# RWKV scan stage: the forward substitution's products on 64 rows instead of 32, a changed order of the work, and eight 128-row products of constants at the head of each pair

## The reference, cut to what matters

```python
def step(s, inp):
    r_t, lw_t, k_t, v_t, a_t, b_t = inp
    sa = jnp.einsum('dbhij,dbhj->dbhi', s, a_t)
    s = s * jnp.exp(lw_t)[..., None, :] + sa[..., None] * b_t[..., None, :] + v_t[..., None] * k_t[..., None, :]
    return s, jnp.einsum('dbhij,dbhj->dbhi', s, r_t)
s_fin, y = lax.scan(step, s0, (tm(r), tm(logw), tm(k), tm(v), tm(a), tm(b)))
```

## Time and profile before

| | us |
|---|---|
| median of 3 runs | 2722.91 |
| lowest and highest run | 2720.70, 2728.16 |
| profiled execution, its own time | 2720.06 |
| its span, first to last instruction | 2718.4 |
| PE busy | 2245.3 (83%) |
| PEld (weight loads) busy | 1735.0 (64%) |
| DVE busy | 984.4 (36%) |
| ACT busy | 518.1 (19%) |

### The profile page before, as it was taken

How to read it: one execution, slowest core, us unless ns; L and a number is a source line. 1 busy time by engine, 2 the same in 40 slices (tenths; PEclk the granted TensorE clock), 3 DMA queues, 4 the chain that set the end, 5 groups by cost and what they waited for, 6 DMA issues and landing times. The chain is left out here.

```text
span 2718.4 us, 39159 instructions
## 1 busy us (share of the span) xinstructions
PE 2245.3 (83%) x16630; PEld 1735.0 (64%) x16630; DVE 984.4 (36%) x2209; ACT 518.1 (19%) x920; POOL 58.2 (2%) x85
## 2 busy tenths in 40 slices
PE   1999955798999886899859993688888889779797
PEld 0888854687888775788624442466666777536445
DVE  3224346411440372675161003544544441120253
ACT  1011022401000101100110003444444333010142
POOL 0000000000000300000000000000000000000000
PEclk9999977898999898899979995776667776689889
DMA  7465410424874321775303203111101111312100
GB/s 289 173 230 228 171 64 8 86 93 165 336 280 155 124 78 37 281 302 217 138 16 109 92 31 125 38 39 38 35 15 39 29 25 41 124 66 93 52 10 16
DMA packets 103014, 305.14 MB, mean 112 GB/s; under 512 B 71352, under 2 KB 79800, under 8 KB 85184
## 3 DMA queue, kind: packets, MB, share of 16 engines
q1 hardware_dynamic: 94384, 225.11, 24.3%
q0 software_dynamic: 8464, 77.60, 7.3%
HBM read 286.88 MB, written 15.80 MB: 111 GB/s over the span
## 5 line engine op out<-in xcount | busy, mean ns | idle before, releaser
L263 PE MATMUL bank<-h,ring 128*128 128x256 f32 x2944 | 646.7, 383 | 22.8 <-DVEq L967 15.3
L263 PEld LDWEIGHTS bank<-h,ring 128*128 128x128 f32 x2944 | 566.3, 193 | 104.0 <-DVEq L967 16.0
L263 PE MATMUL bank<-mixed,ring 128*128 128x512 f32 x384 | 165.0, 592 | 1.3 <-DVE mixed L1249 1.3
L877 PE MATMUL bank<-ffn_hidden,ring 128*128 128x256 f32 x704 | 152.4, 379 | 3.3 <-PEq L903 3.3
L877 PEld LDWEIGHTS bank<-ffn_hidden,ring 128*128 128x128 f32 x704 | 133.6, 190 | 22.2 <-issue 4.1
L263 PEld LDWEIGHTS bank<-mixed,ring 128*128 128x128 f32 x384 | 72.9, 190 | 93.5 <-issue 91.4
L156 DVE CUSTOM_DVE_ANT_0 next_w<-next_w,next_vec,par 128x1024 f32<-128x1024 f32 x96 | 120.1, 1279 | 11.4 <-DMA next_w<-in_mod_stream 11.4
L1987 DVE TENSOR_TENSOR rw_u<-bank,rw_lam 128x128 f32<-128x128 f32 x120 | 35.0, 291 | 236.1 <-PE bank L1660 233.1
L889 DVE SCALAR_TENSOR_TENSOR x<-bank,mod,x 128x256 f32<-128x256 f32 x24 | 10.0, 477 | 231.6 <-PE bank L877 231.6
L1668 PE MATMUL bank<-rw_gr,rw_u 64*64 64x32 f32 x960 | 80.3, 252 | 13.0 <-DVE rw_u L1987 12.9
L1581 PE MATMUL bank<-rw_xa,ring 64*64 64x64 f32 x1024 | 30.5, 305 | 72.2 <-DVE rw_xa L1920 72.2
(11 more groups left out here) (387 smaller groups left out, 3415.1 us busy)
## 6 DMA issues: line engine op xcount, KB each, us to landing
ring<-in_stream SPq DMA_DIRECT2D x89, 2048.0 KB, 8.0
next_w<-in_mod_stream POOLq DMA_DIRECT2D x24, 2048.0 KB, 9.9
ctx<-in_mod_rest POOLq DMA_DIRECT2D x16, 1024.0 KB, 7.3
rwkv_projections<-proj_out POOLq DMA_DIRECT2D x8, 1024.0 KB, 6.7
y<-bias_table SPq DMA_DIRECT2D x48, 128.0 KB, 4.9
rw_rkv<-rwkv_projections SPq DMA_DIRECT2D x8, 768.0 KB, 4.2
rw_at<-rw_at_kept SPq DMA_DIRECT2D x16, 256.0 KB, 3.9
rwkv_o<-rwkv_projections POOLq DMA_DIRECT2D x1, 2048.0 KB, 16.0
```

What stands on the lines that cost most here:

```text
L263: mm = pe.matmul(out, ring_tile(k, n, kt, i * P), rhs[kt], start=start and kt == kts[0], stop=stop and kt == kts[-1])
L877: mm = pe.matmul(k.psum[grp * 4 + i][:, 0:T], ring_tile(k, n, kt, i * P), rhs[part * KT + kt], start=(part == 0 and kt == 0), stop=(part = ...
```

## The change

The solving products take 64 rows. A new tile `LM` for each direction holds the inverse on the partitions `brows(h)` and zeros (set once) on `krows(h)`. The load from DRAM goes into `LM` instead of `BG`, and both operands of L1618's product span `rows64(h)`. `LM` has one copy per direction, so SP waits for the products of the pair before (`pq_up`) ahead of the load. The product with the unit matrix stays on 32 rows. Room for `LM` comes from two small tiles, which now lie on constants (`tri`, `neg`).

In `steps_made` the unit products of both heads come first and then those of `rt` for both heads; their number and size stay.

The order changes by its intervals. A new item `warm` stands at the head of each step from i = -1 on: ten times eight products of 128 rows and 512 columns, of the unit matrix with constants, into the next work bank, which nobody reads.

```diff
+        order += [("warm", i, 1)] if i >= -1 else []
         order += interleave((0, 1, has(i, [("chain", i, c) for c in range(NCK + 1)])),
-                            (0, 0.7, has(i + 1, scan_solve(i + 1))),
-                            (0, 0.3, has(i + 2, scan_grams(i + 2))),
+                            (0, 0.75, has(i + 1, scan_solve(i + 1))),
+                            (0.1, 0.42, has(i + 2, scan_grams(i + 2))),
                             (0, 0.3, has(i - 1, scan_read(i - 1))),
-                            (0.3, 0.36, has(i + 2, [("bonus", i + 2, j) for j in range(2)])),
-                            (0.45, 1, has(i + 2, [("inv", i + 2, s) for s in range(1, LCH)])),
-                            (0.42, 1, has(i + 3, scan_ready(i + 3))))
+                            (0.42, 0.46, has(i + 2, [("bonus", i + 2, j) for j in range(2)])),
+                            (0.55, 1, has(i + 2, [("inv", i + 2, s) for s in range(1, LCH)])),
+                            (0.48, 0.9, has(i + 3, scan_ready(i + 3))))
...
+        LM = [sb(f"lm{d}", 8, 2, LCH) for d in range(2)]
...
+                for d in range(2):
+                    for h in range(2):
+                        nc.vector.memset(LM[d][krows(h)].rearrange("p a b t -> p (a b t)"), 0.0)
...
+                if n:
+                    sp.wait_ge(pq_up, 8 * n)
                 for d in range(2):
                     for h in range(2):
-                        sp.dma_start(BG[n % 3][d][brows(h), :, :, 96:128].rearrange("p c e t -> p (c e) t"),
+                        sp.dma_start(LM[d][brows(h)].rearrange("p c e t -> p (c e) t"),
                                      blocks(mt_dram, n, d, h)).then_inc(mt_in, 16)
...
-                        x, y = VQ[n % 2][d][brows(h), c2, e, :], KP[d][brows(h), c2, e, :]
+                        x, y = VQ[n % 2][d][rows64(h), c2, e, :], KP[d][rows64(h), c2, e, :]
...
-                        mm = pe.matmul(out[brows(h), j * P:(j + 1) * P], BG[n % 3][d][brows(h), c2, e, 96:128], both,
-                                       start=True, stop=True)
+                        mm = pe.matmul(out[brows(h), j * P:(j + 1) * P], LM[d][rows64(h), c2, e, :], both, start=True,
+                                       stop=True)
...
+                elif kind == "warm":
+                    out = take(*item)
+                    for _ in range(8):
+                        pe.matmul(out, ident, k.con[:, 0:512], start=True, stop=True)
```

More of the change, by code:

```diff
@@ L1363, in stage_rwkv_scan @@
         jobs = {"lora": [(0,), (1,)], "gram": [(0,), (1,)], "gr": [(0,), (1,)], "btok": [()],
-                "atok": [()], "akv": [()], "pq": [()],
+                "atok": [()], "akv": [()], "pq": [()], "warm": [()],
                 "kk": [()], "bonus": [()] if item[2:] == (0,) else [],
@@ L1407, in stage_rwkv_scan @@
         U, lam = sb("u", 2, 2, 64), sb("lam", 4, 2, NCK)
-        starts, gmask, sel, half2 = sb("starts", 512), sb("gmask", 64), sb("sel", 512), sb("half2", 6)
-        cen, omka, eps = sb("cen", P), sb("omka", KT), sb("eps", 1)
+        starts, gmask, sel, half2 = sb("starts", 512), const(k, "tri")[:, 0:64], sb("sel", 512), sb("half2", 6)
+        cen, omka, eps = const(k, "neg"), sb("omka", KT), sb("eps", 1)
         kst, kstT, rst, rstT = sb("kst", 8), sb("kstT", P), sb("rst", 8), sb("rstT", P)
@@ L1628, in steps_made @@
                 for h in range(2):
+                    to = [outs[h][rows64(e), 0:384].rearrange("p (c v) -> p c v", c=4) for e in range(2)]
+                    units = [ident[rows64(e), rows64(e)] for e in range(2)]
                     for e in range(2):
-                        unit = ident[rows64(e), rows64(e)]
-                        to = outs[h][rows64(e), 0:384].rearrange("p (c v) -> p c v", c=4)
+                        pe.matmul(to[e][:, :, 0:64], units[e], units[e].unsqueeze(1).to_broadcast([64, 4, 64]), start=True,
+                                  stop=False, skip_group_check=True)
+                    for e in range(2):
                         rt = RT[n % 2][d][rows64(e), 256 * half:256 * half + 256].rearrange("p (c h t) -> p c h t", h=2,
                                                                                            t=LCH)
-                        pe.matmul(to[:, :, 0:64], unit, unit.unsqueeze(1).to_broadcast([64, 4, 64]), start=True, stop=False,
+                        pe.matmul(to[e][:, :, 64:96], units[e], rt[:, :, h, :], start=False, stop=False,
                                   skip_group_check=True)
-                        pe.matmul(to[:, :, 64:96], unit, rt[:, :, h, :], start=False, stop=False, skip_group_check=True)
                 for j in range(4):
```

## The result

| | before | after |
|---|---|---|
| median, us | 2725.53 (4 runs) | 2756.67 (4 runs, 2751.59 to 2766.64) |
| profiled execution, own time and span | 2720.06, 2718.4 | 2757.0, 2755.3 |
| mean granted clock | 0.858 | 0.889 |

The recorded ratio is 1.0136, with a 95% interval of 1.0116 to 1.0157: 1.4% slower, where 2714 us was forecast. (The two medians of the table alone make 1.0114.

A forecast was written before the change was run, and what follows sets the result against it. Each pair was taken as a PE-bound head, partly at half clock, and a tail bound by DVE's inversion. Steady pairs: -4.0, 77.9 us for 81.9; whole stage: -9.1, so 2714 us; range 2700 to 2728, with rivals 2682 to 2748.

The forecast's parts named there:

- I take 7 us cold in all: Head of a steady pair: 7 us still run at half rate, work of 4 at full rate, costing +3.1 us.
- order term: Steady pair: kk 2 sums moved into the PE-bound head cost +1.1 us, `exps` between two pq items +1.0.
- Burst and boundary: Boundary of a steady pair: burst takes 8.9 us; U14 to next U0 goes from 9.1 to 12.2, +3.1.
- rival 4: DVE falls behind: the squeezed inversion costs 2 us in six pairs, giving 2726 us; chance 0.13.
- Clock at the head: Head of a steady pair: warming the 26.3 and 10.2 us cold stretches gives -15.7 us, remaining cold work +3.1.
- rival 2: The burst buys nothing: clock falls again soon after it, some 22 us cold per head, 2752 us; chance 0.24.
- rival 1: The clock stays up: both falls in the head vanish, pair 7 stays warm, 2678 to 2690, say 2684; chance 0.20.
- Solving products: The pq items: on 64 rows, unit and solving products run one after the other, 0.43 us an item, +3.4 a pair.
- Rival 3: The pq items: unit and solving products overlap still, -3.4 us in seven pairs, 2690 us; chance 0.10.
- Ends: Last pairs and read-out: pair 5 +5.2 us, pair 6 +1.1, pair 7 -3, last read-out +4.8.
- Step -1: Before the first pair: burst free behind PE's 16.7 us wait for `elements`, akv items start earlier, -3 us.
- Nothing, for want of a reason: Order of unit products, LM loads with SP's new wait, memsets and banks: claimed to change no time.

The follow-up runs named there:

- e5: Changed kernel with grams (0 to 0.3) and bonus (0.3 to 0.36) back at their old places: 2741.31 us, ratio 1.0078 to the kernel before.
- e6: Changed kernel with the kk items (`ready`) moved later, to 0.58 to 0.97 from 0.48 to 0.9: 2729.02 us, ratio 1.0050 to the kernel before.
- e13: Changed kernel with the product with the unit matrix on 64 rows as well: 2721.35 us, ratio 1.0007 to the kernel before.
- e1: Changed kernel with bursts out and the old order back, leaving solving products on 64 rows: 2716.84 us, ratio 0.9996 to the kernel before.
- e3: Changed kernel without bursts and with solving products on 32 rows, leaving the new order: 2730.24 us, ratio 1.0038 to the kernel before.
- e4: Changed kernel without the ten bursts, new order and 64-row solving products kept: 2728.93 us, ratio 1.0045 to the kernel before.
- e9: Changed kernel without bursts and with the kk items later, at 0.58 to 0.97: 2711.81 us, ratio 0.9966 to the kernel before.
- e15: Changed kernel with order, bursts and 64 rows undone, leaving tile `LM` and the gr item's order: 2727.00 us, ratio 1.0015 to the kernel before.
- e10: Changed kernel with old order and no bursts, solving and unit products both on 64 rows: 2688.50 us, ratio 0.9888 to the kernel before.
- e12: Changed kernel with the kk items later and bursts only at steps -1 to 5: 2711.40 us, ratio 0.9972 to the kernel before.
- e7: Changed kernel with no bursts at the last three heads (pairs 6 and 7, last read-out): 2744.85 us, ratio 1.0099 to the kernel before.
- e2: Changed kernel with the old order and solving products on 32 rows, leaving the ten bursts: 2741.83 us, ratio 1.0079 to the kernel before.
- e16: Changed kernel with late kk items, solving and unit products on 64 rows, bursts only up to head 5: 2687.63 us, ratio 0.9882 to the kernel before.
- e14: Changed kernel with old order and no bursts, unit products on 64 rows, solving products on 32: 2779.92 us, ratio 1.0228 to the kernel before.

## Why the prediction was wrong, point by point

Two steps failed. The clock term "I take 7 us cold in all" was mis-sized: 13.7 to 27.3 us of the heads of pairs 1 to 4 are cold. And the order term (+1.1 and +1.0) prices only what PE, ACT and DVE do; it left out SP's load of the next pair, for which PE waits 2.8 to 6.2 us a pair.

The profiled time was to be 2711.0 (2720.06 less 9.1) and is 2757.0. Of these 46.0 us, pairs 1 to 4 bring 36.5 (348.1 for 311.6), pair 0 4.9 (78.6 for 73.7), the stretch before the first U 4.7, pair 6 1.3 and the end 1.7; pair 5 and 7 came out 2.6 and 0.6 under.

- **Burst and boundary: right.** 8.5 us for 8.9; U14 to U0 11.6 for 12.2 in pair 3. DVE didn't fall behind: U12 to U14 7.7 us for 7.4, so rival 4 is out.
- **Clock at the head: wrong by the most.** "I take 7 us cold in all": it was 27.3 in pairs 3 and 4, 17.1, 17.1 and 13.7 in pairs 0 to 2 and nothing in pair 5. By the prediction's own rate, 27.3 - 7 = 20.3 us more at half rate are 20.3 x 3/7 = 8.7 us. This is rival 2, near the place that it named: the clock fell 0.7 us ahead of the akv items and stayed down through them, the chain item and the sums. It gave 2752. That this is near the measured time is in part luck: it has nothing of the load, the 64 rows did help the clock, and the run that it blamed (akv, akv, chain, sums) ends at a fall only in pair 2 (8.4 us behind U0, for 3.4 us). The trace had told of it in the earlier trace rows, where 10.20 of 10.20 busy us were cold; the working used that row against rival 1 and then spared the head all the same. What the engine did before each fall is below.
- **Order: a step left out.** The text priced what PE, ACT and DVE do in moved items and asked of SP only what the new wait does. It never asked what SP's own load of the next pair stands behind. That is 3.0 us of wait in pair 3 (0.26 before), in the text nothing; e5 and e6 put it at 16 to 23 us of the time with all that follows from it. The rows to look at were SP's timeline: load issued at 1968.00, wanted at 1973.97, and 4.5 us to land (2070.53 to 2075.07 after) leave 1.4 us of slack, against items moved by 0.1 of an 81.9 us step. Two more waits of PE are new in the head and were priced at nothing: 1.40 us for the read-out's `rw_ysb` and 1.23 us for `elements` (rows in the last section). Three old ones, 0.68, 0.84 and 0.68 us, are gone or shorter; PE's idle time from U0 to U12 of pair 3 is 6.0 us for 2.5. Whether the terms for `kk` and `exps` (+1.1 and +1.0) were right no run tells.
- **Solving products: mechanism right, price nearly so, a gain missed.** They do run one after the other: 0.54 us an item for 0.43 (1.54 less 1.00), so 4.3 a pair for 3.4. Rival 3 is out for this kernel. e13 shows what it is worth, 35 us, with what the clock does then. What the text didn't have is that 64 rows raise the clock at all ("64 rows don't lift it" was part of rival 2). The two cancel in e1.
- **Sum of pair 3.** 77.9 + 8.7 (clock) + 3.0 (load) + 0.9 (items) - 0.6 (boundary) = 89.9, and 88.6 were measured. Over pairs 1 to 4 the same terms give 24.6 + 15.7 + 3.6 - 1.2 = 42.7 us on top of the forecast, and 36.5 were measured. They account for the miss to some 6 us; as the waits just named are not in them, they are an estimate and no proof.
- **Ends: nearly right.** Pair 5 +2.6 (+5.2), pair 6 +2.4 (+1.1), pair 7 from U0 to U14 -3.6 (-3), the last read-out +6.5 (+4.8).
- **Step -1: wrong way.** The first U was to come 3 us earlier and came 1.7 later (1779.31 for 1777.59). The late load is in this step too: PE waits 7.60 us for ACT's square, for 1.30 before. With neither bursts nor the old order (e3, e4) the first U is at 1777.9. With the kk items later it is at 1774.9 with bursts (e6) and 1775.3 without (e9), but in e5, where that wait is down to 1.78 us, it is at 1780.1. No run took this stretch apart.
- **"Nothing, for want of a reason": not contradicted** for tile `LM` and the gr products (e15, within 0.4%).

By the Trainium skill ("TensorE: Matmul & The Clock Gate", Part 3) products overlap when their row groups differ, and its table of packings has products side by side in different columns too. This case's traces agree with the first for 32 and 32 rows (1.00 us) and with the second for two 64-row kinds on the same rows, whose outputs lie on different partitions (`krows(h)` and `brows(h)`) and so in different columns (e10, 1.01 us). The mix, however, has different columns as well and runs one behind the other (1.54 us); there the measurement decides, and the prediction's low end, "other columns of the array may be enough", fails for it.

What stays open: why e4 plus bursts loses 25 us when e9 plus bursts (e12) loses none. 10 of it are the last three bursts (e7). The rest goes with the wait, which is there in the one and not in the other, but no run took it apart further. Nor did any run tell what lets the clock fall, or why taller products keep it up.

## What to carry to other kernels

When items of a hand-made order move, list for every queue, SP's included, what stands behind them and by when it is wanted; a load with 1.4 us of slack doesn't survive a shift of 5. When a product is made taller, make those that ran beside it as tall: here that one line was worth 28 to 35 us; it took the whole change back to even (e13), and without the bursts and the new order it makes a kernel 1.1% faster than the one before (e10). Work added to lift the clock has to be held against what it displaces, place by place. The bursts came out even in pairs 2 to 4 of e2 and as a whole in e12 and e16; in the changed kernel they cost 25 us, 10 of them at the end.

## What the runs showed of the hardware that was not expected

- Products of 32 and of 64 rows on shared rows run one after another, whichever is the taller (1.54 us an item in e1 and e14). Two kinds with the same number of rows overlap, on disjoint rows (1.00 us before) and on shared ones (1.01 us in e10).
- A product on 64 rows, half of them meeting zeros, takes PE as long as one on 32 (0.62 and 1.06 us for the same passes in e1 and e14), and the granted clock of the same stretch was higher with it: 0.77 for 0.72, 0.89 for 0.73.
- 8.5 us of dense 128-row passes did not by themselves keep the clock up for the head behind them. In pair 3 it fell to 1.2 GHz three times before U12, and each time PE had just been idle or was so: 1.40 us until 2030.73 (fall at 2032.4), 1.23 us until 2059.53 (2059.7), 2.99 us until 2075.85 (2073.4).

```profile
2030.73 0.35 PE L1669 MATMUL bank<-rw_u,rw_gr 64*64 64x64 f32 x5 [1.40 <-DVE rw_ysb L2013]
...
2059.53 1.86 PE L1588 MATMUL bank<-rw_xa,ring 64*64 64x64 f32 x64 [1.23 <-DVE rw_xa L1933]
```

Once down it stayed so with PE busy for 13.70 of 13.70 us. Such a gap was neither enough nor needed, though. Pairs 1 and 5 have the same gap of 1.40 us behind U0 and one of 1.24 and 1.30 us near 24, and there the clock stayed up until 38.0 and 55.1 us behind U0. And in the kernel before it fell at 1998.69 with PE busy throughout, behind chain and sums items; so it did in pairs 0, 1, 3 and 4. Pair 1 of the changed kernel, then the kernel before on both sides of that fall (columns as in the earlier trace rows):

```profile
1857.90:1895.80 37.90, 33.28 (x737) 26.32 (x737) 18.51 (x36) 18.83 (x34) 0.00 (x0) 1.00 0.20 36
```

```profile
1985.10:1998.60 13.50, 13.50 (x294) 10.86 (x291) 6.91 (x27) 5.25 (x11) 0.00 (x0) 1.00 0.02 4
1998.70:2000.00 1.30, 1.30 (x31) 1.30 (x26) 1.23 (x4) 0.00 (x0) 0.00 (x0) 0.50 0.00 0
```

The Trainium skill ("TensorE: Matmul & The Clock Gate", section "HAM oscillation — how this bites in real kernels") puts the fall down to gaps in which PE idles, there long waits for a DMA; the section behind it, "A second HAM failure mode: psum-queue depth-cycling", has short gaps between groups of products do the same. The three falls of pair 3, with gaps of 1.2 to 3.0 us, fit the second; the fall at 1998.69 fits neither, and there the measurement decides. The prediction was right not to rest on the gap rule alone. No run took a single gap away and left the rest, so it isn't shown what a gap does to the clock.
